# An expert layer: token-block layout, more row buffers, all dot products before the second half, both one-hots in one operation

## What is computed

```python
def peer(xn, wq, keys, u, v):        # xn: (tokens, D); keys: (8, 2, 128, 64); u, v: (16384, D)
    q = (xb @ wq).reshape(128, 8, 2, 64)                      # per block of 128 tokens
    s1, s2 = einsum(q[:, :, 0], keys[:, 0]), einsum(q[:, :, 1], keys[:, 1])
    v1, i1 = top_k(s1, 16); v2, i2 = top_k(s2, 16)
    sc, ci = top_k(all 256 sums v1 + v2, 16)
    e = i1[ci // 16] * 128 + i2[ci % 16]                      # 8 x 16 experts for a token
    g = softmax(sc)
    hid = einsum('thkd,td->thk', u[e], xb)
    return einsum('thk,thkd->td', gelu(hid) * g, v[e])
h = h + peer(rmsnorm_2(h, norm2_w), ...);  out = rmsnorm_2(h, final_norm_w)
```

## Time and profile before

| | us |
|---|---|
| median of 3 runs | 3227.78 |
| lowest, highest | 3227.45, 3239.96 |
| the profiled execution | 3228.97 |
| its span, first to last instruction | 3227.2 |

### The profile page before, as it was taken

How to read it: one execution, slowest core, us unless ns; L and a number is a source line. 1 busy time by engine, 2 the same in 40 slices (tenths; PEclk the granted TensorE clock), 3 DMA queues, 4 the chain that set the end, 5 groups by cost and what they waited for, 6 DMA issues and landing times.

```text
span 3227.2 us, 42908 instructions
## 1 busy us (share of the span) xinstructions
PE 3095.4 (96%) x15287; PEld 2602.1 (81%) x15287; DVE 1869.7 (58%) x3650; ACT 1112.8 (34%) x1807; POOL 1875.0 (58%) x1796
## 2 busy tenths in 40 slices
PE   8999999999999999999999999999999989889898
PEld 6777888887678888887778889989999967667776
DVE  7674545236854441514732367788688667666666
ACT  3455222113732220213542123434466423222323
POOL 7423766666256666765435665768644556555553
PEclk9999999999999999999999999999999989999999
DMA  6111222223122222222121224778766799888885
GB/s 226 66 40 40 98 100 96 92 100 109 40 72 92 105 92 96 100 98 79 53 72 67 104 87 168 279 253 311 275 246 242 266 363 350 316 319 324 334 317 218
DMA packets 154238, 540.83 MB, mean 168 GB/s; under 512 B 11172, under 2 KB 64581, under 8 KB 117701
## 3 DMA queue, kind: packets, MB, share of 16 engines
q1 hardware_dynamic: 39168, 285.23, 24.6%
q0 software_dynamic: 36864, 134.23, 11.1%
q10 hardware_dynamic: 78020, 118.84, 10.6%
HBM read 480.08 MB, written 58.18 MB: 167 GB/s over the span
## 4 chain that ended last, share of the span: by engine, by line
PE 74%; DMA 11%; DVE 5%; POOL 4%; issue 3%; ACT 2%; ACTq 0%; DVEq 0%; POOLq 0%; SPq 0%
PE banks L194 64%; DMA memory<-in_peer_v,memory 8%; POOL weights_split L3177 3%; DMA memory<-in_peer_u,memory 2%; PE banks L2748 2%; PE banks L2174 1%; PE banks L2212 1%; POOL memory L3171 1%; ACT weights_split L3021 1%; ACT memory L3062 1%; DMA weights_raw<-in_weights 1%; PE banks L1110 1%; DVE memory L2948 1%; PE banks L1197 1%; PE banks L1169 1%
## 5 line engine op out<-in xcount | busy, mean ns | idle before, releaser
L194 PE MATMUL banks<-memory,weights_split 128*128 128x512 f32 (+1 forms) x9456 | 2071.3, 376 | 26.7 <-DVE memory L555 11.1
L194 PEld LDWEIGHTS banks<-memory,weights_split 128*128 128x128 f32 x9456 | 1714.5, 188 | 305.5 <-issue 45.9
L3305 POOL TENSOR_SCALAR weights_split<-weights_raw 128x512 fp32r<-128x512 f32 x576 | 376.2, 663 | 786.6 <-PE banks L194 393.2
L3310 POOL TENSOR_TENSOR weights_split<-weights_raw,weights_split 128x512 fp32r<-128x512 f32 x576 | 771.0, 1350 | 0.0
L3177 POOL TENSOR_TENSOR weights_split<-weights_raw,weights_split 128x512 fp32r<-128x512 f32 x384 | 496.8, 1317 | 457.6 <-ACT weights_split L3021 456.4
L194 PE MATMUL banks<-weights_split,memory 128*128 128x512 f32 (+1 forms) x2880 | 679.2, 398 | 62.0 <-DVE memory L2954 36.3
L194 PEld LDWEIGHTS banks<-weights_split,memory 128*128 128x128 f32 x2880 | 550.9, 195 | 186.7 <-issue 41.2
L3021 ACT ACTIVATE weights_split<-weights_raw 128x1024 fp32r<-128x1024 f32 x256 | 269.4, 1053 | 73.7 <-DMA weights_raw<-in_weights 35.9
L2828 DVE SCALAR_TENSOR_TENSOR banks<-memory,memory,banks 128x1024 f32<-128x1024 f32 x127 | 163.1, 1285 | 151.3 <-DMA memory<-in_peer_v,memory 149.7
L2820 DVE CUSTOM_DVE_ANT_0 memory<-memory,banks 128x1024 f32<-128x1024 f32 x128 | 155.0, 1215 | 120.1 <-DMA memory<-in_peer_u,memory 119.9
L3123 ACT ACTIVATE memory<-memory 128x384 fp32r<-128x384 f32 x128 | 67.2, 525 | 406.3 <-DVE memory L2948 397.7
(11 more groups left out here) (278 smaller groups left out, 2718.2 us busy)
## 6 DMA issues: line engine op xcount, KB each, us to landing
weights_raw<-in_weights SPq DMA_DIRECT2D x272, 1024.0 KB, 4.8
hidden<-memory ACTq DMA_DIRECT2D x64, 384.0 KB, 4.3
routing<-memory ACTq DMA_DIRECT2D x12, 2048.0 KB, 7.4
memory<-routing ACTq DMA_DIRECT2D x32, 768.0 KB, 7.0
memory<-hidden ACTq DMA_DIRECT2D x32, 768.0 KB, 12.0
window_rows<-memory ACTq DMA_DIRECT2D x1, 3064.0 KB, 25.7
chunk_rows<-memory ACTq DMA_DIRECT2D x1, 2556.0 KB, 10.8
residual<-in_x ACTq DMA_DIRECT2D x4, 512.0 KB, 8.7
```

Source lines behind the costliest of these rows:

```text
L194: last = k.nc.tensor.matmul(out, left[a], right[b], start=start and n == 0, stop=stop and n == 2, skip_group_check=True)
L3305: k.nc.gpsimd.tensor_scalar(cut(high, n * PIECE, PIECE), cut(raw, n * PIECE, PIECE), 1.0, 1.0, ALU.mult, ALU.mult).then_inc(k.high_made, 1)
L3310: k.nc.gpsimd.tensor_tensor(cut(low, n * PIECE, PIECE), cut(raw, n * PIECE, PIECE), cut(high, n * PIECE, PIECE).bitcast(F32), ALU.subtract ...
```

## The change

- The queries are stored by token block and then head, and the layer's operand by token block and then tile, so that the place of one block is free as a whole once its scores (or, for block 3, its operand) are used.
- There are 5 row buffers from the start (the two of before and three places of block 3), 6 for rows 0 to 11, 7 to row 32 and 8 to row 127; for the v rows eleven, for the last 24 of them seven. GpSimd's goal is 4 to 6 rows beyond the plan in the u phase and 8 in the v phase.
- All 128 dot products stand in the u phase (22 in each of three routes, 50 among the matrices, 12 before the gates). The Gelu of their results stands at v unit 0, and the v rows are spread over v units 1 to 123.
- Both one-hots of a group come from one `tensor_tensor` of 2 x 4 x 128 elements. The shares are multiplied in behind it: in two groups of three by ScalarE, with four operations of 128 elements, in every third by VectorE, with one of 512.
- The matrix product writes its four tokens interleaved in the bank (every fourth element); the copy reads the bank in order and writes runs of four.
- Scores, exponentials, turns, matrices and loads stand at later units (matrices in units 89 to 122 instead of 85 to 120, loads from 125 instead of 124). The final gain row is loaded at v unit 123 instead of before v unit 0.

The diff, cut to its core (lines of three dots mark what is left out):

```diff
     lists = 2 * PEER_HEADS
     ORDER = [DENSE_BLOCKS] + list(range(DENSE_BLOCKS))
-    SCORE_AT, EXP_AT, TURN_AT = [0, 8, 27, 47], [15, 37, 59, 81], [None, 43, 65, 84]
-    MATRIX_FIRST, MATRIX_COUNT, LOAD_AT = 85, 36, 124
-    IN_ROUTE, IN_MATRIX, BEFORE_GATES = [0, 20, 22, 22], 20, 14
-    BEFORE_VALUES = sum(IN_ROUTE) + IN_MATRIX + BEFORE_GATES
-    DOTS, DOTTED_AT, VALUES_AT, SPARSE_END = P, 24, 26, 123
-    EARLY = 30
+    DOTS = P
+    SCORE_AT, EXP_AT, TURN_AT = [0, 8, 27, 50], [15, 38, 60, 82], [None, 45, 67, 88]
+    MATRIX_FIRST, MATRIX_COUNT, LOAD_AT = 89, 34, 125
+    IN_ROUTE, IN_MATRIX, BEFORE_GATES = [0, 22, 22, 22], 50, 12
+    assert sum(IN_ROUTE) + IN_MATRIX + BEFORE_GATES == DOTS
+    SPARSE_END = 123
 
     def planned(unit):
 
 
-        marks = [(19, 0), (39, 20), (61, 42), (83, 64), (121, 84), (PEER_KEYS, BEFORE_VALUES),
-                 (PEER_KEYS + DOTTED_AT, DOTS), (PEER_KEYS + VALUES_AT, DOTS), (PEER_KEYS + SPARSE_END, 2 * DOTS)]
+        marks = [(19, 0), (42, 22), (64, 44), (86, 66), (122, 116), (PEER_KEYS, DOTS), (PEER_KEYS + 1, DOTS),
+                 (PEER_KEYS + SPARSE_END, 2 * DOTS)]
         if unit <= marks[0][0]:
             return 0
         for (u0, c0), (u1, c1) in zip(marks, marks[1:]):
@@ -2569,7 +2569,7 @@
...
-        rows, cols = [k.take(BATCH * P) for _ in range(DEPTH)], [k.take(BATCH * P) for _ in range(DEPTH)]
+        hots = [k.take(2 * BATCH * P) for _ in range(DEPTH)]
...
-        gathered += [k.take(D_MODEL) for _ in range(4)]
+        of_block = [k.take(D_MODEL) for _ in range(BLOCKS)]
     with k.scope(at=HN_AT):
-        gain_row, results, squares = k.take(D_MODEL), [k.take(D_MODEL) for _ in range(2)], [k.take(512) for _ in range(2)]
-        gathered += [k.take(D_MODEL) for _ in range(4)]
-        assert k.pointer <= SMALL_AT
-    FIRST, QUERY, LAST = (0, 1), (2, 3, 4, 5), (5, 6, 7, 8, 9)
+        parts = [k.take(D_MODEL) for _ in range(2 * BLOCKS)]
+    with k.scope(at=HN_AT):
+        gain_row, results = k.take(D_MODEL), [k.take(D_MODEL) for _ in range(2)]
+    with k.scope(at=HN_AT + 16 * KB):
+        squares = [k.take(512) for _ in range(2)]
+    gathered += [of_block[DENSE_BLOCKS], parts[DENSE_BLOCKS], parts[BLOCKS + DENSE_BLOCKS]]
+    ALWAYS = list(range(len(gathered)))
+    gathered += of_block[0:DENSE_BLOCKS]
+    ASKED = ALWAYS + list(range(len(ALWAYS), len(gathered)))
+    gathered += [parts[5], parts[6]]
+    LATE = ALWAYS + [len(gathered) - 2, len(gathered) - 1]
+    AFTER_HIDDEN = len(gathered) - 2
+    gathered += [parts[0], parts[1], parts[2], parts[4]]
+    APPLIED = LATE + list(range(len(gathered) - 4, len(gathered)))
+    TAIL_FREE = 2 * DOTS - 24
...
+    def by_block(x):
+        return x.rearrange("p (b t) -> p b t", t=P)
+
+    def hn_tile(side, n):
+        half = cut(hn.memory, side * D_TILES * TOKENS, D_TILES * TOKENS)
+        return half.rearrange("p (b k t) -> p k b t", b=BLOCKS, k=D_TILES)[:, n]
+
+    def by_scalar(g):
+        return g % 3 != 2
...
-        if i < EARLY:
-            homes.append(FIRST[i % 2])
-        elif i < BEFORE_VALUES:
-            homes.append((FIRST + QUERY)[i % 6])
+        if i < DOTS:
+            homes.append(ASKED[i % (6 if i < 12 else 7 if i < 33 else 8)])
+        elif i < TAIL_FREE:
+            homes.append(APPLIED[(i - DOTS) % len(APPLIED)])
         else:
-            homes.append((FIRST + LAST)[(i - BEFORE_VALUES) % 7])
+            homes.append(LATE[(i - TAIL_FREE) % len(LATE)])
...
-                          queries[half, h * TOKENS + b * P:h * TOKENS + (b + 1) * P],
+                          queries[half, (b * PEER_HEADS + h) * P:(b * PEER_HEADS + h + 1) * P],
...
-            pe.wait_ge(rows_ready, g + 1)
-            pe.wait_ge(cols_ready, g + 1)
+            if by_scalar(g):
+                pe.wait_ge(scaled, BATCH * sum(by_scalar(n) for n in range(g + 1)))
+            else:
+                pe.wait_ge(weighted, sum(not by_scalar(n) for n in range(g + 1)))
             if g >= 2:
                 pe.wait_ge(matrix_copied, g - 1)
             else:
                 pe.wait_ge(emptied, 3 * DENSE_BLOCKS)
+            by_key = score_banks[g % 2].memory.rearrange("p (n t) -> p t n", t=BATCH)
             for t in range(BATCH):
-                s = slice(t * P, (t + 1) * P)
-                last = mm(score_banks[g % 2].memory[:, s], rows[g % DEPTH][:, s], cols[g % DEPTH][:, s], start=True,
-                          stop=True, skip_group_check=True)
+                last = mm(by_key[:, t, :], cut(hots[g % DEPTH], t * P, P), cut(hots[g % DEPTH], (BATCH + t) * P, P),
+                          start=True, stop=True, skip_group_check=True)
...
-            for t in range(BATCH):
-                at = g * BATCH + t
-                last = v.tensor_scalar(rows[g % DEPTH][:, t * P:(t + 1) * P], iota, cut(turned, at, 1),
-                                       cut(turned, 2 * DENSE + at, 1), ALU.is_equal, ALU.mult)
-            last.then_inc(rows_ready, 1)
-            v.tensor_tensor(cols[g % DEPTH].rearrange("p (t n) -> p t n", t=BATCH),
-                            iota.unsqueeze(1).broadcast_to(three),
-                            cut(turned, DENSE + g * BATCH, BATCH).unsqueeze(2).broadcast_to(three),
-                            ALU.is_equal).then_inc(cols_ready, 1)
+            both = [P, 2, BATCH, P]
+            v.tensor_tensor(hots[g % DEPTH].rearrange("p (s t n) -> p s t n", s=2, t=BATCH),
+                            iota.unsqueeze(1).unsqueeze(1).broadcast_to(both),
+                            turned[:, 0:2 * DENSE].rearrange("p (s t) -> p s t", s=2)[
+                                :, :, g * BATCH:(g + 1) * BATCH].unsqueeze(3).broadcast_to(both),
+                            ALU.is_equal).then_inc(hot, 1)
+
+        def weigh_rows(g):
+            rows = cut(hots[g % DEPTH], 0, BATCH * P).rearrange("p (t n) -> p t n", t=BATCH)
+            dve.wait_ge(hot, g + 1)
+            v.tensor_tensor(rows, rows, cut(shares, g * BATCH, BATCH).unsqueeze(2).broadcast_to(three),
+                            ALU.mult).then_inc(weighted, 1)
...
+            if not by_scalar(g):
+                weigh_rows(g)
...
+                        act.wait_ge(emptied, 3 * DENSE_BLOCKS)
+                        a.activation(shares, cut(turned, 2 * DENSE, DENSE), ACT.Copy).then_inc(iota_placed, 1)
...
-            by_token = staging[portion % 2].rearrange("p (j t) -> p t j", t=PORTION)
+            by_key = staging[portion % 2].rearrange("p (j t) -> p j t", t=PORTION)
             act.wait_ge(made, g + 1)
             at = g % per_portion * BATCH
-            a.activation(by_token[:, at:at + BATCH, :],
-                         score_banks[g % 2].memory.rearrange("p (t n) -> p t n", t=BATCH),
+            a.activation(by_key[:, :, at:at + BATCH],
+                         score_banks[g % 2].memory.rearrange("p (n t) -> p n t", t=BATCH),
...
+        def scale_rows(g):
+            act.wait_ge(hot, g + 1)
+            for t in range(BATCH):
+                row = cut(hots[g % DEPTH], t * P, P)
+                a.activation(row, row, ACT.Copy, scale=cut(turned, 2 * DENSE + g * BATCH + t, 1)).then_inc(scaled, 1)
...
+            for g in matrix_after.get(n + 1, ()):
+                if by_scalar(g):
+                    scale_rows(g)
         for p in range(2):
             act.wait_ge(hidden_written[p], 16 * (SLOTS // 2))
-        act.dma_start(gain_row, k.dram["final_row"]).then_inc(gain_in, 16)
         for e in range(PEER_KEYS):
             if e == 0:
-                act.wait_ge(eaten, BEFORE_VALUES)
+                act.wait_ge(eaten, DOTS)
+                a.activation(applied, hid, ACT.Gelu).then_inc(weighed, 1)
+            if e == SPARSE_END:
+                act.wait_ge(eaten, max(i for i in range(2 * DOTS) if homes[i] > LATE[-1]) + 1)
+                act.dma_start(gain_row, k.dram["final_row"]).then_inc(gain_in, 16)
             act.wait_ge(multiplied, e + 1)
             if e >= 4:
                 act.wait_ge(used, e - 3)
             a.activation(operand_high(e % 4), gated[e % 2], ACT.Copy).then_inc(high_made, 1)
             if e >= 3:
                 unit_split(PEER_KEYS + e)
-            if e == DOTTED_AT:
-                act.wait_ge(eaten, DOTS)
-                a.activation(applied, hid, ACT.Gelu).then_inc(weighed, 1)
...
-            if i == EARLY:
-                pool.wait_ge(scored, 2 * BLOCKS)
-            if home >= 6 and uses[i] == 1:
-                hidden_banks[-1].await_filled(pool)
+            if uses[i] == 1:
+                if home == 2 or home in ASKED[len(ALWAYS):]:
+                    pool.wait_ge(scored, 2 if home == 2 else 2 * (home - len(ALWAYS)) + 4)
+                if home in (3, 4):
+                    pool.wait_ge(tokens_turned, 1)
+                if home >= AFTER_HIDDEN:
+                    hidden_banks[-1].await_filled(pool)
...
-            ahead = 1 if unit < 50 else 4
-            seen = unit - 3 if unit < PEER_KEYS else unit
```

(8 more changed lines are left out.)

32 lines of the change are left out of this document (16 added, 16 removed).

## The result

The changed kernel took 3129.84 us (median of 4 runs, 3127.38 to 3131.42); the kernel before took 3232.31 in the runs beside it. The ratio is 0.968, with a 95% interval of 0.9656 to 0.9704: 3.2% faster. Forecast were 3145 us, and 3118 to 3205. The profiled execution of the changed kernel has a span of 3128.3 us against 3227.2, 98.9 less.

A forecast was written before the change was run, and what follows sets the result against it. TensorE matmuls were taken to bound the kernel, with fetch latency, not bandwidth, costing 85 us in the v phase. Terms -73.0 - 8.3 - 9.6 + 3 + 4.2 = -83.7 gave 3145 us, range 3118 to 3205.

The forecast's parts named there:

- v phase: Last layer's second half, 128 units: longer fetch lead and fewer rows a unit bring 4.77 us a unit to 4.2, -73.0 us.
- 20.64 us: v phase, kernel before: one pass of the loop of low half, fetch, DMA, VectorE, ScalarE, which the fetch lead must cover.
- Matrix stretch: Units with one-hot products: TensorE's waits on ScalarE's copy of the matrix go, VectorE stays hidden, scalings just hidden; -8.3 us.
- The copy's 585: Matrix stretch: ScalarE's copy, 1093 ns before, taken at 585 ns because it now writes runs of four.
- Stall at unit 50: u phase: the burst of fetches ahead of the low halves disappears, TensorE's idle and slower matmuls with it; -9.6 us.
- The +3 for rows 12 and 33: u phase: GpSimd may wait where the buffer cycle changes length; charged +3 us, 0 to 10.
- Border: Between u and v phases: load, held issue and store wait move one unit; +4.2 us, between -8 and +8.
- Layout, at nothing: Queries and operand stored by token block: runs of 128 elements remain, no cost; 3 us if each three-run read cost 1 ns.
- Rival A: Matrix stretch: writing every fourth PSUM element slows the one-hot matmuls, 97 us in all, 3242 us; chance 0.12.
- Rival B: v phase: weight loads queue behind rows and land at 13.5 us, 4.6 us a unit, 3196 us; chance 0.14.
- C: u phase: GpSimd's fetches wait for VectorE before full buffers two or three times, 10 us each, 3165 to 3175; chance 0.11.
- D: v phase: the lead does not help, VectorE's order or TensorE's operand buffers hold 4.77 us a unit, 3218; chance 0.07.

## Why the prediction was right, point by point

- **v phase, -73.0 forecast, -85.7 measured.** It runs at 4.08 us a unit from the second sixteen units on: under the 4.2 I chose, and under the bound of 4.106, which I had divided out of a piece of the chain that counts the last matmul whole and holds one short gap. The bandwidth part held: 352 GB/s were asked and up to 379 moved, without a wait. The waits that I named were not all: besides the 36.3 us for the operand, TensorE waited 25.8 us for low halves of weights, which VectorE makes in order with the rows, and some 30 us went by the lower clock. The reason was half the story. That the lead was too short is shown by the kernel before with a lead of 7. But I took "20.64 us" as given, and used the density of rows only for bandwidth and for VectorE's load, while fewer rows and no u rows, at the old lead, gain 72 us too.

```profile
PE banks L194 <- DVE weights_split L2962: 25.8, 12, 4.1
```

- **Matrix stretch, -8.3 forecast, -10.7 measured** (units 80 to 126). The copy's 585 came out at 597. A unit with three groups spent 3.17 us on its products and the waits between them and spends 2.72, 0.45 less where I had counted 0.35. The scalings are 305 ns each in a row, above both bounds of 200 and 291, and still just hidden; the changed kernel's timeline for one unit of three groups leaves 0.37 us:

```profile
2401.98 1.05 ACT L3049 ACTIVATE weights_split<-weights_raw 128x1024 fp32r<-128x1024 f32 x1
2402.93 2.44 ACT L3102 ACTIVATE memory<-memory,memory 128x128 f32<-128x128 f32 x8
2405.74 0.49 ACT L3070 ACTIVATE memory<-banks 128x384 f32<-128x384 f32 x1 [0.37 <-PE banks L194]
```

- **Stall at unit 50, -9.6 forecast; -9.7 in units 32 to 63,** and -8.7 us of the whole, alone, in the kernel before. The +3 for rows 12 and 33 did not come.
- **Border, +4.2 forecast, +7.8 measured,** within its bounds, but not by the one unit's shift that I gave as the reason. ScalarE is held no longer in issuing the three loads (6.99 + 9.96 + 3.21 us, before 9.97 + 4.14 + 7.64). What is new is that it stands from 2555.2 to 2558.39 before the last routing store, which before had landed 3 us ahead of the first load, and that the last hidden store takes 10.34 us to land instead of 7.44. The transfers are fuller there, 405 GB/s in the first 25 us; that this is the cause is likely and not shown. TensorE, busy for 8.87 of the second 25 us, has a granted clock of 0.57 in them. The 3.6 us too little here and the 3 us too much in the u phase cancel, which is luck.
- **Layout, at nothing.** Units without matrices take 4.18 us before and after, sixteen of them 66.9 us in both.
- **Rival A** (spaced writes into PSUM) is out: 94.9 us packed and spaced. The sentence of the Trainium skill (SBUF — State Buffer, Door 1: The DMA port swizzle) on PSUM, which speaks of matmuls, does not hold for these fp32 ones. The sentence on SBUF agrees: ScalarE's copy takes 1097 ns with the writes 128 bytes apart against 598 in runs of four. **Rival B** did not come: the weights' landing rose from 7.1 us to 8.4 in the v phase, under the 11 that I had worked out:

```profile
weights_raw<-in_weights SPq DMA_DIRECT2D x62, 1024.0 KB, 8.4
```

- **C** did not come: GpSimd's fetches wait 6.6 us for VectorE between 1930 and 2560 us, 3.5 at most, where they waited 20.3 and 5.9. **D** is refuted by the kernel before with the longer lead.

So the direction, the places and the order of the terms held. The size was 15 us short of the truth, of which 12.7 lie in the v phase's pace.

## What to carry to other kernels

Before rows are rebuilt to need fewer buffers or less work, change the number that says how far ahead they are fetched: here one constant gave 68 of 103 us. When a loop of engines is compared with a lead, take its length at the load that the kernel will have, and expect two remedies for one bottleneck to overlap, not to add. A queue that holds its engine in issuing, while the DMA share is at 1, need not be what costs the time: here the first load itself landed late, and moving the issue of the others gained nothing. And look at both sides of a loss, the waits and the matmuls that run at the lower clock behind them: they were 55 and 30 us here.
